# Attention scores of six heads by two stacked high/low products, with keys reloaded through DRAM in pieces

## The chip, the cores and the metric

The kernel runs on one core of a Trainium2 chip. The metric is device time in microseconds of one execution. The names of the engines are those of the profile: PE is TensorE (PEld its weight loads), DVE is VectorE, ACT is ScalarE, POOL is GpSimd, SP is the queue that issues most DMAs.

## The reference

A two-layer trunk on 1040 tokens (16 meta tokens and 1024 of input) of width 1024. The first layer has two groups of heads side by side; the change touches the first of them, eight heads of 64 with sparse attention:

```python
s = jnp.einsum('bqhd,bsd->bqhs', qib, k_idx)              # indexer of 16 heads picks the keys
score = jnp.einsum('bqhs,bqh->bqs', jax.nn.relu(s), wb)
_, idx = lax.top_k(jnp.where(causal, score, -inf), 256)
logits = einsum(q, k[idx]) * 64 ** -0.5 - slopes[h] * dist  # ALiBi
p = softmax(where(valid, logits, -inf)); out = einsum(p, v[idx])
```

The second group (HGRN2, eight heads of 64) is a gated linear recurrence over chunks. Both outputs go through one projection `w_out`, then DeepNorm layer norms, SwiGLU, and a second layer with pooling. Everything is in float32.

## The kernel before

Three stages follow one another with a barrier between them: `projection` (x by `w_in`, indexer scores, selection of 256 keys as a mask of distances, to about 466 us), `mixers` (both head groups and `w_out`, about 467 to 932 us) and `trunk` (all the rest). Selection is a mask, so the attention multiplies the queries of a tile with all keys up to it.

`mixers` walks nine tiles of queries: tile 0 has 16 rows, tiles 1 to 8 have 128 each, and tile m sees `NKEYS[m]` keys (16, 144, 272, 400, 528, 656, 784, 912, 1040). Each tile has eight steps, one for a head of attention (`units`) and at the same time one level of the recurrence. The order on every engine is written out in loops over `steps`; a step (m, h) puts on PE:

- `qk`: logits of head h (L1260), 128 queries by up to 1024 keys in float32, the head's 64 rows padded with zeros to 128 in `qaT` since `kaT` holds two heads in 128 rows; in tile 8 `qk_rest` does the last 16 keys;
- `gram` (L1303, L1293 at h = 0): products of the recurrence's level;
- a job in the `SHARED` bank of PSUM: `share` (h = 2, L1235), then `meta`, `out`, `kT`, `state`, `qa` for h = 0 to 4, `ot_rec` for h = 6. `qa` makes the queries of the next tile (L1196); in tile 0 it is spread over h = 0 to 3. Each use of the bank waits for `shared_done` of the use before it;
- `turn` (L1317): transposes of the probabilities of the head before; `pv_pair` (L1330) at odd h; a quarter of the output projection (`op`, L1253) at odd h.

DVE adds the mask to the logits and takes the maximum (`masked`, L1544; the next `qk` waits for `nmax_raw`), and copies the recurrence's products into `S`. ACT does the exponentials, the gates and most copies out of PSUM. POOL does `carry` (L1135, L1139): after `gram` of level h it scales `qp` and `key`, and `gram` of level h + 1 waits for it. `pT` has three buffers (`TS = 3`). SP's queue loads `z`, `q`, `v`, `g`, weights of `w_out` and rows of `y` in a written order. While PE has little to do in tile 0, `stream` issues products that nobody reads (L1349).

```python
            for a in range(0, min(NKEYS[m], 1024), 512):
                last = scores_of(m, h, a, min(512, NKEYS[m] - a), a)
            last.then_inc(qk_done, 1)
```

Of the kernel before, what the change touches and what calls it, by code (L numbers as in the profile page):

```python
# [12 lines left out]
P = 128  # L13
D = 1024
# [44 lines left out]
LEVELS = 7  # L59
SLOPES = [2.0 ** (-8.0 * (h + 1) / A_HEADS) for h in range(A_HEADS)]  # L60
# [23 lines left out]
def build(nc, ins, out):  # L84
# [3 lines left out]
    with ExitStack() as top:  # L88
# [19 lines left out]
        qz_dram = nc.dram_tensor("qz_scratch", [2, 4, P, L], F32, kind="Internal").ap()  # L108
        vg_dram = nc.dram_tensor("vg_scratch", [2, L, A_WIDTH], F32, kind="Internal").ap()
# [11 lines left out]
        with ExitStack() as heads:  # L121
            with ExitStack() as mixer:
# [6 lines left out]
                kaT = sb(mixer, "kaT", [P, 4, L])  # L129
                va = sb(mixer, "va", [P, NT, A_WIDTH])  # L130
                with stage() as c:
                    projection(nc, c, sem, sb, banks, ident, x, meta, w_in_v, ins, score, cqT, kaT, va, y, qz_dram, vg_dram, kiT, masks, w_qa0)
                with stage() as c:
                    mixers(nc, c, sem, sb, banks, ident, x, meta, ins, score, masks, w_qa0, cqT, kaT, va, y, qz_dram, vg_dram, raw, draw)
# [6 lines left out]
def projection(nc, c, sem, sb, banks, ident, x, meta, w_in_v, ins, score, cqT, kaT, va, y, qz_dram, vg_dram, kiT, masks, w_qa0):  # L141
# [75 lines left out]
    link = sem("dve_link")  # L217
    iota_done, w_qa_loaded, w_qa_scaled = sem("iota_done"), sem("w_qa_loaded"), sem("w_qa_scaled")
# [89 lines left out]
    def _(sp):  # L308
# [23 lines left out]
        for j, (col, _, _, _) in enumerate(SLABS):  # L332
            if j == 0:
                sp.wait_ge(x_transposed, NT)
            if j >= 2:
                sp.wait_ge(slab_hi, j - 1)
                sp.wait_ge(slab_lo, j - 1)
            if j == len(SLABS) - 2:
                sp.wait_ge(sc_psum, len(units))
            sp.dma_start(slab_raw(j), w_in_v[:, :, col:col + SW]).then_inc(slab_loaded[j % 2], 16)  # L340
            if j == len(SLABS) - 2:
                sp.dma_start(w_qa0, ins["w_uq"][0].rearrange("(k p) f -> p k f", p=P)).then_inc(w_qa_loaded, 16)

# [448 lines left out]
def mixers(nc, c, sem, sb, banks, ident, x, meta, ins, score, masks, w_qa0, cqT, kaT, va, y, qz_dram, vg_dram, raw, draw):  # L792
# [33 lines left out]
    u = sb(c, "u", [P, W])  # L826
    lnw = sb(c, "lnw", [P, W])
# [8 lines left out]
    q_past = sb(c, "q_past", [P, W])  # L836
# [4 lines left out]
    wq_last = [buf[:, i * DC * QW:(i + 1) * DC * QW].rearrange("p (k f) -> p k f", k=DC)  # L841
               for buf in (va[:, :, :].rearrange("p m f -> p (m f)"), kaT[:, :, :].rearrange("p f t -> p (f t)"))
               for i in range(2)]
# [28 lines left out]
    q_joined = sem("q_joined")  # L872

# [7 lines left out]
    def shared_job(m, h):  # L881
        jobs = {0: ("meta", m - 1), 1: ("out", m - 1), 2: ("kT", m - 1), 3: ("state", m - 1), 4: ("qa", m + 1), 6: ("ot_rec", m - 1)}
# [4 lines left out]
    def share_job(m, h):  # L887

        return m - 1 if h == 2 and 1 <= m <= NT else None

# [19 lines left out]
    assert shared_job(0, 4) == ("qa", 1) and not any(shared_job(0, h) for h in range(STEPS) if h != 4)  # L910
# [61 lines left out]
    def _(sp):  # L972
# [44 lines left out]

        load_z(0)
        load_q(0)
        sp.dma_start(w_qa[:, :, :], w_qa0).then_inc(w_loaded, 16)  # L1020
# [15 lines left out]
        for m in range(5):  # L1036
            load_y(m)
        for m, h in steps:
            if h == 0 and 1 <= m < NT - 1:
                load_q(m + 1)  # L1040
            if h == 5 and 1 <= m < NT:
# [8 lines left out]
            if (m, h) == (NT, 0):  # L1050
                sp.wait_ge(qk_done, NU)
                sp.wait_ge(qk_tail, A_HEADS)
            if (m, h) == (NT, 2):
# [1424 lines left out]
```

## Time and profile before

| what | value |
|---|---|
| median of 3 runs | 2519.51 us (2513.75 to 2519.68) |
| the profiled execution: its own time | 2521.23 us |
| span in its trace | 2519.4 us |
| PE busy | 2432.4 us (97%) |
| PE weight loads busy | 2081.2 us (83%) |
| DVE, ACT, POOL busy | 1177.1, 962.6, 1051.1 us |

The table reads: PE has something in flight nearly always, the other engines half of the time or less. Matmuls overlap in the array, so the distance between two starts tells the price of a product, not the duration in the row. The page cuts the span into 40 slices of 63 us; `mixers` fills slices 8 to 15.

### The profile page before, as it was taken

Reading aid. Unit: us, or ns where it says so; the run is one execution under the profiler, and the core shown is the slowest. Engines: PE = TensorE matmul, PEld = TensorE weight load, DVE = VectorE, ACT = ScalarE, POOL = GpSimd, SP = SyncE. Lnnn points to the kernel's source line nnn. Section 1 sums busy time; section 2 is a strip of 40 time slices with the busy share of each in tenths; the row PEclk is TensorE's granted clock in tenths of the full one; section 3 lists DMA queues with packets and bytes.
Section 4 is the critical chain, followed back from the end, with each engine's and each line's share of the span. In section 5 each row is a group of like instructions: output and inputs, shape, how many; then the busy total and the mean of one; then the engine's idle time right before and its main releaser. Section 6 shows DMA issues by size and latency. Waiting matters only on the chain.

```text
span 2519.4 us, 35989 instructions
## 1 busy us (share of the span) xinstructions
PE 2432.4 (97%) x13958; PEld 2081.2 (83%) x13958; DVE 1177.1 (47%) x2304; ACT 962.6 (38%) x1630; POOL 1051.1 (42%) x584
## 2 busy tenths in 40 slices
PE   7899999989999989999999999999999999999996
PEld 7889999767788779899898888888888888888885
DVE  6788985444455523333333466323355432232224
ACT  3677783334444324222223433322333322332222
POOL 0433123255554424443444544544544444455442
PEclk9999999899999999999999999999999999999998
DMA  4101330333333333333232323233233333333331
GB/s 140 34 18 35 100 100 31 105 97 114 101 113 106 103 111 117 92 101 97 72 101 84 100 71 114 84 117 89 79 101 101 87 97 101 100 101 103 115 101 42
DMA packets 275002, 231.42 MB, mean 92 GB/s; under 512 B 10769, under 2 KB 255569, under 8 KB 274833
## 3 DMA queue, kind: packets, MB, share of 16 engines
q1 hardware_dynamic: 266640, 220.59, 29.3%
q10 hardware_dynamic: 8192, 8.52, 1.0%
q8 instruction: 112, 1.84, 0.3%
q14 instruction: 58, 0.47, 0.1%
HBM read 215.81 MB, written 12.71 MB: 91 GB/s over the span
## 4 chain that ended last, share of the span: by engine, by line
PE 58%; DMA 1%; POOL 1%; ACT 1%; issue 1%; DVE 1%; POOLq 0%; SPq 0%; ACTq 0%; DVEq 0%
PE banks L2080 37%; PE banks L2114 19%; PE banks L2146 1%; DMA last_draw<-in_w_down 1%; POOL wL L2016 1%; PE banks L1801 1%; POOL dL L2023 1%; DMA cq_raw<-in_w_up 0%; PE banks L2105 0%; PE banks L2108 0%; PE banks L2132 0%; ACT wH L2192 0%; ACT dH L2198 0%; DVE y L2338 0%; ACT hH L1811 0%
## 5 line engine op out<-in xcount | busy, mean ns | idle before, releaser
L2016 POOL TENSOR_TENSOR wL<-cq_raw,wH 128x2048 fp32r<-128x2048 f32 x87 | 407.9, 4688 | 527.0 <-ACT wH L2192 527.0
L2080 PE MATMUL banks<-hL,wH 128*128 128x512 f32 (+1 forms) x1760 | 619.0, 352 | 7.7 <-ACT hid L2207 5.0
L2080 PE MATMUL banks<-hH,wL 128*128 128x512 f32 (+1 forms) x1760 | 618.1, 351 | 0.0
L2080 PE MATMUL banks<-hH,wH 128*128 128x512 f32 (+1 forms) x1760 | 616.1, 350 | 0.0
L2080 PEld LDWEIGHTS banks<-hL,wH 128*128 128x128 f32 x1760 | 331.3, 188 | 57.0 <-ACT hid L2207 6.3
L2312 DVE TENSOR_TENSOR hid<-hid,banks 128x512 f32<-128x512 f32 (+1 forms) x110 | 64.3, 584 | 656.3 <-PE banks L2080 554.8
L2080 PEld LDWEIGHTS banks<-hH,wL 128*128 128x128 f32 x1760 | 331.2, 188 | 46.3
L2080 PEld LDWEIGHTS banks<-hH,wH 128*128 128x128 f32 x1760 | 331.8, 189 | 45.0
L2023 POOL TENSOR_TENSOR dL<-last_draw,dH 128x1024 fp32r<-128x1024 f32 x88 | 220.2, 2502 | 313.7 <-ACT dH L2198 313.7
L2338 DVE TENSOR_TENSOR y<-y,banks 128x512 f32<-128x512 f32 (+1 forms) x340 | 231.9, 686 | 183.4 <-PE banks L2114 182.1
L2198 ACT ACTIVATE dH<-last_draw 128x1024 fp32r<-128x1024 f32 x88 | 93.3, 1060 | 498.7 <-PE banks L2114 321.3
L2114 PE MATMUL banks<-dH,hidL 128*128 128x512 f32 x704 | 278.8, 396 | 2.3 <-issue 2.3
L2114 PE MATMUL banks<-dL,hidH 128*128 128x512 f32 x704 | 277.9, 395 | 0.0
L2114 PE MATMUL banks<-dH,hidH 128*128 128x512 f32 x704 | 277.7, 394 | 0.0
L2209 ACT ACTIVATE hidH<-hid 128x512 fp32r<-128x512 f32 (+1 forms) x110 | 60.4, 549 | 384.7 <-DVE hid L2312 384.7
L2192 ACT ACTIVATE wH<-cq_raw 128x2048 fp32r<-128x2048 f32 x87 | 166.1, 1909 | 49.8 <-DMA cq_raw<-in_w_up 39.0
L2114 PEld LDWEIGHTS banks<-dH,hidL 128*128 128x128 f32 x704 | 132.5, 188 | 34.7 <-issue 2.7
L2114 PEld LDWEIGHTS banks<-dH,hidH 128*128 128x128 f32 x704 | 132.6, 188 | 31.3
L2114 PEld LDWEIGHTS banks<-dL,hidH 128*128 128x128 f32 x704 | 132.6, 188 | 30.5
L1135 POOL TENSOR_TENSOR qp<-qp,tot 64x256 f32<-64x256 f32 x112 | 77.2, 689 | 182.3 <-PE banks L1303 177.9
L501 PE MATMUL banks<-shared,hH 128*128 128x256 f32 (+1 forms) x648 | 136.9, 280 | 0.0
L501 PE MATMUL banks<-shared,hL 128*128 128x256 f32 (+1 forms) x432 | 120.7, 280 | 0.0
(278 smaller groups left out, 4074.8 us busy)
## 6 DMA issues: line engine op xcount, KB each, us to landing
cq_raw<-in_w_gate SPq DMA_DIRECT2D x88, 512.0 KB, 4.7
cq_raw<-in_w_up SPq DMA_DIRECT2D x88, 512.0 KB, 6.0
last_draw<-in_w_down SPq DMA_DIRECT2D x88, 512.0 KB, 3.4
w_out_part<-in_w_out SPq DMA_DIRECT2D x60, 512.0 KB, 4.0
va<-in_w_in SPq DMA_DIRECT2D x10, 1024.0 KB, 5.3
va<-in_x SPq DMA_DIRECT2D x8, 512.0 KB, 4.5
vg_scratch<-y ACTq DMA_DIRECT2D x32, 128.0 KB, 1.7
y<-in_x SPq DMA_DIRECT2D x8, 512.0 KB, 8.0
```

The source lines that it names most:

```text
L501: last = nc.tensor.matmul(banks[0:n, bank, 0:SW], h[:, k, a:a + n], w[:, k, :], start=first, stop=stop)
L1135: nc.gpsimd.tensor_tensor(late, late, blocks[r, :, 0, :].to_broadcast([HD, n, 2 ** l]), ALU.mult)\
L1801: last = self.nc.tensor.transpose(self.banks[:, self.bank_of(i), k * P:k * P + n], self.y[0:n, m, kk * P:(kk + 1) * P], self.ident[0:n, 0:n])
L2016: nc.gpsimd.tensor_tensor(wL[:, ff % 2, :, :, :].rearrange("p g k f -> p (g k f)"), raw[:, :, :, :].rearrange("p g k f -> p (g k f)"), wH[ ...
L2023: nc.gpsimd.tensor_tensor(dL[:, ff % 2, :], draw, dH[:, ff % 2, :].bitcast(F32), ALU.subtract)\
L2080: last = nc.tensor.matmul(banks[:, GU + (2 * q + g) % 3, 0:n], wt[:, ff % 2, g, k, :], h[:, k, a:a + n], start=(k == 0 and part == 0), sto ...
L2114: last = nc.tensor.matmul(banks[0:n, DN + num % 3, :], h[:, (2 * g + u) % 3, t0 - ph.t0:t0 - ph.t0 + n], wt[:, u, (j % 2) * 512:(j % 2 + 1 ...
L2192: nc.scalar.activation(wH[:, ff % 2, :, :, :], raw[:, :, :, :], ACT.Copy).then_inc(w_hi, 2)
L2198: nc.scalar.activation(dH[:, ff % 2, :], draw, ACT.Copy).then_inc(d_hi, 1)
L2209: nc.scalar.activation(hidH[:, ff % 3, a - ph.t0:a - ph.t0 + n], hid[:, q % 2, 0:n], ACT.Copy)\
L2312: nc.vector.tensor_tensor(hid[:, q % 2, 0:n], hid[:, q % 2, 0:n], banks[:, GU + (2 * q + 1) % 3, 0:n], ALU.mult)\
L2338: nc.vector.tensor_tensor(at, at, banks[0:n, DN + num % 3, :], ALU.add).then_inc(y_added, 1)
```

## The change

Six of the eight heads get their logits from two products in the reduced-width type fp32r. A head's key rows (64) are stored twice in 128 rows: the high part (rounded to fp32r) and the rest. The queries are also stored as two stationary matrices: `q_parts[0]` has the high part of q in both halves, `q_parts[1]` the rest of q over the half that meets the high keys and zero in the other. Two heads stay as they were, with `whole_keys`. The stacked keys of six heads need more room than `kaT`, and a shift across partitions, so the keys go to DRAM in `projection` and come back in `mixers`: the first 144 keys of six heads before the stage's end, the other 896 in three pieces of two heads, which ACT rounds (`keys_high`) and DVE subtracts (`keys_low`) at the steps (0,6), (1,1) and (1,4). Space is made by `TS = 2`, by `q_past` in `u`, and by other places for the last weights of `w_out`. The job `qa` is split in two (`qa` at h = 4, `qb` at h = 5), with the low parts made by DVE; `share` moves behind `qk` and `gram`.

```diff
+def load_keys(sp, raw_keys, k_dram, heads, at, signal):
+    for par in range(2):
+        for half in range(2):
+            sp.dma_start(raw_keys[HD * half:HD * (half + 1)].rearrange("p (f two) t -> p two f t", two=2)[:, par],
+                         k_dram[heads[0] // 2:heads[1] // 2, HD * par:HD * (par + 1), at].rearrange("f p t -> p f t")).then_inc(signal, 16)
...
+            if j == 6:
+                sp.wait_ge(slab_out, FILL_UNITS)
+                for f in range(4):
+                    sp.dma_start(k_dram[f], kaT[:, f, :]).then_inc(keys_stored, 16)
...
+        load_keys(sp, first, k_dram, (0, SPLIT_HEADS), slice(0, FIRST_KEYS), first_keys)
+        sp.wait_ge(first_keys, 64)
...
-    TS = 3
+    TS = 2
...
+    def piece_at(m, h):
+        return {(0, 6): 1, (1, 1): 2, (1, 4): 3}.get((m, h))
...
+        def load_piece(piece):
+            sp.wait_ge(k_split, piece)
+            part, heads, at = keys_in(piece)
+            load_keys(sp, part, k_dram, (heads.start, heads.stop), at, k_loaded)
+
         load_z(0)
         load_q(0)
+        sp.dma_start(whole_keys[:, :, :], k_dram[SPLIT_HEADS // 2:].rearrange("f p t -> p f t")).then_inc(kw_loaded, 16)
...
-        for m in range(5):
+        for m in range(3):
             load_y(m)
+        load_piece(1)
         for m, h in steps:
             if h == 0 and 1 <= m < NT - 1:
                 load_q(m + 1)
+            if piece_at(m, h) and piece_at(m, h) + 1 < KEY_PIECES:
+                load_piece(piece_at(m, h) + 1)
+            if (m, h) == (1, 7):
+                sp.wait_ge(k_split, KEY_PIECES)
+                load_y(3)
+                load_y(4)
...
+            if h < SPLIT_HEADS:
+                return nc.tensor.matmul(logits[0:n, at:at + kn], q_parts[:, part, h, 0:n], keys[:, h, a:a + kn],
+                                        start=(part == 0), stop=(part == 1))
...
+            if (m, h) == (0, 0):
+                pe.wait_ge(k_split, 1)
+            if m == 2 and h % 2 == 0 and h < SPLIT_HEADS:
+                pe.wait_ge(k_split, h // 2 + 2)
...
         for i, (m, h) in enumerate(steps):
-            if share_job(m, h) is not None:
-                on_shared("share", share_job(m, h))
             if i < NU:
                 qk(i)
...
             if m == 0 and h < 4:
-                on_shared("qa", 1, h)
                 stream(1)
-            if shared_job(m, h) and h and m:
+            if share_job(m, h) is not None:
+                on_shared("share", share_job(m, h))
+            if shared_job(m, h) and h:
                 on_shared(*shared_job(m, h))
...
+        def keys_high(piece):
+            if piece:
+                act.wait_ge(k_loaded, 64 * piece)
+            part, heads, at = keys_in(piece)
+            nc.scalar.activation(keys[:, heads, at], part, ACT.Copy).then_inc(k_hi, 1)
...
-            early = shared_job(m, h) if h == 3 else None
+            early = shared_job(m, h) if h in (3, 5) else None
...
+            if piece_at(m, h):
+                keys_high(piece_at(m, h))
...
+        def queries_low(what, m):
+            dve.wait_ge(q_hi, 1 if m == 0 else 2 * m + (what == "qb"))
...
+            last.then_inc(shared_done, 1)
```

PE in tile 4, steps 2 and 3, before. `rsums` is `share`, `ident,key` the job `kT`, `ident,probs` is `turn`; `k_tok` is the job `state`.

```order
L1235 MATMUL banks<-ident,rsums 64x128 x8
L1260 MATMUL banks<-kaT,qaT 128x512
L1260 MATMUL banks<-kaT,qaT 128x16
L1303 MATMUL banks<-qp,key 128x128 x4
L1204 MATMUL banks<-ident,key 128x128 x4
L1317 MATMUL banks<-ident,probs 128x128 x4
L1260 MATMUL banks<-kaT,qaT 128x512
L1260 MATMUL banks<-kaT,qaT 128x16
L1303 MATMUL banks<-qp,key 128x128 x4
```

The same place in the changed kernel, from `qk` of step 2 to `turn`:

```order
L1333 MATMUL banks<-keys,q_parts 128x512
L1333 MATMUL banks<-keys,q_parts 128x16
L1333 MATMUL banks<-keys,q_parts 128x512
L1333 MATMUL banks<-keys,q_parts 128x16
L1394 MATMUL banks<-qp,key 128x128 x4
L1308 MATMUL banks<-ident,rsums 64x128 x8
L1277 MATMUL banks<-ident,key 128x128 x4
L1408 MATMUL banks<-ident,probs 128x128 x4
```

`share` has moved from ahead of `qk` to right ahead of `kT`, which uses the same bank.

ACT at the end of tile 0 before, from the fifth head's exponentials of 16 rows:

```order
L1444 ACTIVATE tot<-lnw 128x512
L1404 ACTIVATE meta_probs<-probs 16x16
L1395 ACTIVATE probs,sums<-probs,nmax 16x16
L1404 ACTIVATE meta_probs<-probs 16x16
L1395 ACTIVATE probs,sums<-probs,nmax 16x16
L1404 ACTIVATE meta_probs<-probs 16x16
L1395 ACTIVATE probs,sums<-probs,nmax 128x144
```

The same place now; `keys<-y` is `keys_high(1)`:

```order
L1536 ACTIVATE tot<-lnw 128x512
L1494 ACTIVATE meta_probs<-probs 16x16
L1485 ACTIVATE probs,sums<-probs,nmax 16x16
L1585 ACTIVATE keys<-y 128x2x896
L1494 ACTIVATE meta_probs<-probs 16x16
L1485 ACTIVATE probs,sums<-probs,nmax 16x16
L1494 ACTIVATE meta_probs<-probs 16x16
L1485 ACTIVATE probs,sums<-probs,nmax 128x144
```

The copy of the first piece stands ahead of the last head's exponentials of tile 0 and of all of tile 1.

## Rows read from the trace of the kernel before

**Rows 1.** The page, part 1: busy us, share of the span, instructions.
```profile
PE 2432.4 (97%) x13958; PEld 2081.2 (83%) x13958; DVE 1177.1 (47%) x2304; ACT 962.6 (38%) x1630; POOL 1051.1 (42%) x584
```
**Rows 2.** Windows: us, busy us (instructions) by engine, PE clock, DMA share, GB/s.
```profile
490.00:510.00 20.00, 18.50 (x103) 17.42 (x102) 7.31 (x21) 5.26 (x20) 12.01 (x19) 0.51 0.42 145
510.00:528.00 18.00, 14.08 (x97) 10.06 (x96) 7.77 (x22) 8.20 (x30) 13.31 (x22) 0.98 0.21 57
```
**Rows 3.** Timeline of PE in tile 8: start, us, row.
```profile
853.32 1.88 PE L1260 MATMUL banks<-kaT,qaT 128*128 128x512 f32 x4
855.04 1.05 PE L1303 MATMUL banks<-qp,key 128*128 128x128 f32 x8
```
**Rows 4.** Timeline of PE in the indexer and in the trunk, fp32r products.
```profile
168.27 0.34 PE L477 MATMUL banks<-kiL,qiT 128*128 128x392 f32 x1
168.45 0.34 PE L479 MATMUL banks<-kiH,qiT 128*128 128x392 f32 x1
...
1499.61 0.39 PE L2114 MATMUL banks<-dH,hidL 128*128 128x512 f32 x1
1499.84 0.39 PE L2114 MATMUL banks<-dL,hidH 128*128 128x512 f32 x1
```
**Rows 5.** Timeline of PE, tile 4, from the op of step 1 to gram of step 3.
```profile
628.30 3.62 PE L1253 MATMUL banks<-w_out_part,oT 128*128 128x256 f32 x16
632.51 1.09 PE L1235 MATMUL banks<-ident,rsums 128*64 128x128 f32 x16 [0.58 <-DVE y L1630]
633.53 1.25 PE L1260 MATMUL banks<-kaT,qaT 128*128 128x512 f32 x4
634.63 1.16 PE L1303 MATMUL banks<-qp,key 128*128 128x128 f32 x8
635.63 0.60 PE L1204 MATMUL banks<-ident,key 128*128 128x128 f32 x4
636.06 0.60 PE L1317 MATMUL banks<-ident,probs 128*128 128x128 f32 x4
636.50 1.15 PE L1260 MATMUL banks<-kaT,qaT 128*128 128x512 f32 x4
638.40 1.13 PE L1303 MATMUL banks<-qp,key 128*128 128x128 f32 x8 [0.75 <-POOL key L1139]
```
**Rows 6.** Timeline of POOL at the same place: carry of level 2.
```profile
635.87 1.57 POOL L1135 TENSOR_TENSOR qp<-qp,tot 64x256 f32<-64x256 f32 x2 [9.79 <-PE banks L1303]
637.52 0.74 POOL L1139 TENSOR_TENSOR key<-key,tot 128x256 f32<-128x256 f32 x1
```
**Rows 7.** Waits of PE by line, 528 to 894 us: total, times, longest.
```profile
PE banks L1303 <- POOL key L1139: 4.8, 7, 1.5
PE banks L1235 <- DVE y L1630: 4.1, 7, 0.6
```
**Rows 8.** Timeline of PE, tile 4, steps 4 and 5.
```profile
646.37 1.14 PE L1303 MATMUL banks<-qp,key 128*128 128x128 f32 x8
647.35 1.95 PE L1196 MATMUL banks<-cq_raw,w_qa 128*128 128x128 f32 x16
...
650.57 1.14 PE L1303 MATMUL banks<-qp,key 128*128 128x128 f32 x8
...
653.60 3.72 PE L1253 MATMUL banks<-w_out_part,oT 128*128 128x256 f32 x16
```
**Rows 9.** Windows around the end of tile 0, columns as in rows 2.
```profile
482.00:494.00 12.00, 8.62 (x58) 6.33 (x57) 5.37 (x28) 6.46 (x25) 6.33 (x14) 0.85 0.93 300
494.00:496.00 2.00, 2.00 (x11) 2.00 (x11) 0.50 (x1) 0.31 (x2) 1.91 (x4) 0.50 1.02 402
```
**Rows 10.** Timeline: first product of tile 1 on PE; a copy into fp32r on ACT.
```profile
489.66 0.48 PE L1260 MATMUL banks<-kaT,qaT 128*128 128x144 f32 x2 [0.79 <-DVE nmax L1544]
...
245.94 1.92 ACT L514 ACTIVATE shared<-va 128x2048 fp32r<-128x2048 f32 x1 [0.46 <-ACT y L538]
```
**Rows 11.** Timeline of DVE: an operation of two operands in SBUF, 1024 elements.
```profile
847.26 1.22 DVE L1761 TENSOR_TENSOR y<-y,n_g 128x1024 f32<-128x1024 f32 x1
```

More of the change, by code:

```diff
@@ L909, in mixers @@
     shared = [("qa", 0)]
-    assert shared_job(0, 4) == ("qa", 1) and not any(shared_job(0, h) for h in range(STEPS) if h != 4)
+    assert shared_job(0, 4) == ("qa", 1) and not any(shared_job(0, h) for h in range(STEPS) if h not in (4, 5))
     for step in steps:
@@ L1189, in on_shared @@
             t0, n = TILES[m]
-            if what == "qa":
+            if what in ("qa", "qb"):
                 if m == 1:
@@ L1193, in on_shared @@
                 w = w_qa if m else w_qa0
-                for ft in q or range(4):
+                for ft in range(4) if m == 0 else range(2) if what == "qa" else range(2, 4):
                     for k in range(QC):
@@ L1238, in on_shared @@
                 last = quarter(m, *q, SHARED)
-            if what != "qa" or not q or q[-1] == 3:
-                last.then_inc(shared_psum, 1)
+            last.then_inc(shared_psum, 1)
         def quarter(m, q, bank):
@@ L1270, in qk @@
                     pe.wait_ge(nmax_tail, tails(i - 1))
-            for a in range(0, min(NKEYS[m], 1024), 512):
-                last = scores_of(m, h, a, min(512, NKEYS[m] - a), a)
+            for part in range(parts_of(h)):
+                for a in range(0, min(NKEYS[m], 1024), 512):
+                    last = scores_of(m, h, a, min(512, NKEYS[m] - a), a, part)
             last.then_inc(qk_done, 1)
@@ L1278, in qk_rest @@
             pe.wait_ge(nmax_raw, i + 1)
-            scores_of(m, h, 1024, NKEYS[m] - 1024, 0).then_inc(qk_tail, 1)
+            for part in range(parts_of(h)):
+                last = scores_of(m, h, 1024, NKEYS[m] - 1024, 0, part)
+            last.then_inc(qk_tail, 1)
         def gram(m, h):
@@ L1449, in off_shared @@
             src = banks[:, SHARED, :]
[L1450 to L1456 removed]
+            if what in ("qa", "qb"):
+                if m:
+                    act.wait_ge(qk_done, A_HEADS * (m - 1) + (4 if what == "qa" else 6))
+                if what == "qb" or m == 0:
+                    if m == 0:
+                        act.wait_ge(dve_pads, 3)
+                    for par in range(2):
+                        r = slice(HD * par, HD * (par + 1))
+                        nc.scalar.activation(q_whole[r, m % 2, par, 0:n], four(src)[r, 3, 0:n], ACT.Copy)
+                for par in range(2):
+                    r, other = slice(HD * par, HD * (par + 1)), slice(HD * (1 - par), HD * (2 - par))
+                    for to in (r, other):
+                        last = nc.scalar.activation(q_part(what, m, 0, par)[to], q_source(what, m)[r], ACT.Copy)
+                last.then_inc(q_hi, 1)
+                return
             if what == "share":
@@ L1489, in _ @@
             gates(0, stage)
+        keys_high(0)
         off_shared("qa", 0)
@@ L1568, in turned, with keys_low @@
                                       banks[:, T_HI, 0:k * P].rearrange("p (f t) -> p f t", f=k)).then_inc(t_dve, 1)
+        def keys_low(piece):
+            dve.wait_ge(k_hi, piece + 1)
+            part, heads, at = keys_in(piece)
+            for par in range(2):
+                r = slice(HD * (1 - par), HD * (2 - par))
+                k = keys[r, heads, at].rearrange("p (f two) t -> p two f t", two=2)[:, par]
+                raw_k = part[r].rearrange("p (f two) t -> p two f t", two=2)[:, par]
+                last = nc.vector.tensor_tensor(k, raw_k, k.bitcast(F32), ALU.subtract)
+            last.then_inc(k_split, 1)
+        def queries_low(what, m):
+            dve.wait_ge(q_hi, 1 if m == 0 else 2 * m + (what == "qb"))
+            if m == 0:
+                dve.wait_ge(dve_pads, 2)
+            for par in range(2):
+                r = slice(HD * par, HD * (par + 1))
+                last = nc.vector.tensor_tensor(q_part(what, m, 1, par)[r], q_source(what, m)[r],
+                                               q_part(what, m, 0, par)[r].bitcast(F32), ALU.subtract)
+            last.then_inc(shared_done, 1)
         def inverted(m):
```

102 lines of the change are left out of this document (74 added, 28 removed).

## The prediction

> **What bounds the kernel now.** I read the page's busy times first [rows 1]: PE has work in 97% of the span, the others in less than half, so a shorter product on PE is worth its time unless something else is late at that place. The change touches `mixers` alone (467 to 932 us), so the rest was read there. The windows [rows 2] show that this is not one regime: from 490 to 510 us, which is tile 1, the granted clock is 0.51 (the 1.2 GHz level) while PE is recorded busy for 18.50 of 20 us; later in tile 1 it is 0.98 and PE is busy for 14.08 of 18. The timeline of PE [rows 5, 8] shows the large tiles: products stand end to end and PE waits for 0.6 or 0.7 us at two places of a tile. The waits by line say how often: seven times for POOL's `carry` and seven times for a DVE addition ahead of `share`, 4.8 and 4.1 us over tiles 2 to 8 [rows 7]. So tiles 2 to 8 are bound by PE with a POOL chain close behind, tile 0 by handovers, tile 1 by a slow clock and by POOL.
>
> **The product.** A score against 1024 keys in float32 takes 855.04 - 853.32 = 1.72 us from start to start [rows 3], 1.68 ns for a key. The indexer's products are of the new kind, high and low keys in fp32r with other weights each time: 0.18 us for 392 columns, and 0.23 us for 512 in the trunk [rows 4], 0.45 ns for a column. Two of them cost 0.91 ns for a key, so 0.77 ns is saved. Tiles 2 to 8 see 272 + 400 + 528 + 656 + 784 + 912 + 1040 = 4592 keys; by six heads and 0.77 ns this is 21.2 us. Not shown is an fp32r product of 16 or 144 columns (tiles 4, 5 and 8 have 36). In tile 4, 528 keys take 634.63 - 633.53 = 1.10 us [rows 5], of which 0.86 is 512 keys, so a product of 16 columns takes 0.12 now. It could cost nothing or, if short ones run at float32's pace, 0.24 for 144 columns: minus 4 to plus 2 us in all. I take 0.11, the row's: tile 4's score then takes 2 x 0.23 + 2 x 0.11 = 0.68 us, 0.42 less.
>
> **Steps 2 and 3: `share` moves.** In tile 4 it takes 10.10 us from the `op` at 628.30 to `gram` of step 3 at 638.40 [rows 5]. New order: op 3.62, score 0.68, gram 1.00, share 1.02, a new wait, kT 0.43, turn 0.44, score 0.68. The new wait: `kT` uses the bank of `share`, so it waits for ACT's copy of it; behind `kT` in PE's queue stand `turn` and the next score. The old cover (score and gram between the two) is gone. Its price isn't shown; the nearest is the wait behind a DVE operation, 0.58 us [rows 5]; an ACT copy of 512 elements is about a quarter of 1.92 us [rows 10] plus a fixed part. I take 0.9, with 0.5 and 1.3 as ends. Sum 8.8 us, so 1.3 is gained, of which 0.84 are the two scores. Is POOL late next? It needs 638.40 - 634.63 = 3.77 us from gram to gram [rows 5, 6]; the new order has 1.00 + 1.02 + 0.9 + 0.43 + 0.44 + 0.68 = 4.5 us of work there. So both old waits go (8.9 us) and 7 x 0.9 = 6.3 comes: plus 2.6 us over seven tiles.
>
> **Steps 4 and 5: `qa` in halves.** Here POOL is late next. From gram to gram it is 650.57 - 646.37 = 4.20 us now, with all of `qa` (1.8) inside [rows 8]. With half of it and a shorter score PE has 1.00 + 0.9 + 0.44 + 0.68 = 3.0 us, less than POOL's 3.77. So 0.43 is gained and 0.9 (`qb`) put behind. The `op` that stands 7.23 us behind gram 4 now [rows 8] then also waits for `qb`'s way out: six small ACT copies (about 1.3) and two DVE operations (0.5) behind its end at 3.77 + 1.0 + 0.9 = 5.7, which gives 7.7 to 7.9. Against the full saving of two scores (0.84) tile 4 gives back about 1.1; tiles 2 and 3 about 1.5 each, tiles 5 to 7 0.9 down to 0.4, tile 8 has no such job. I take 5.5 us, ends 3 and 8.
>
> **Steps 0 and 1.** `gram` 1 waits for two DVE copies behind gram 0, and `out` for a chain on ACT that begins at the score of step 0; the first score's saving moves these, the second's hardly. I take 2.5 us given back, ends 0 and 4. ACT gets later by the moved `share`, so that `state` waits in tiles 2 and 3: 0.8. Tiles 2 to 8: 21.2 + 2.6 - 5.5 - 2.5 - 0.8 = 15 us gained, ends 8 and 21.
>
> **Tiles 0 and 1: the pieces.** ACT takes `keys_high(1)` at the end of step (0,6) and stands there until the piece has landed; behind it in its queue are the last exponentials of tile 0 and all of tile 1, and DVE, then PE, wait for them. When does it land? SP issues it behind v, two weight halves, two norm rows and three tiles of y: 0.26 + 1.05 + 1.05 + 1.11 MB, with the piece's 0.92 (128 x 1792 x 4 bytes) 4.39 MB. The queue moved 300 GB/s for 12 us and 402 for 2 [rows 9], 3.60 + 0.80 = 4.40 MB by 496.0 us. Then come the copy of 1792 elements at 1.92/2048 [rows 10], 1.7 us, two DVE operations of 896 at 1.22/1024 [rows 11], 2.1 us, and a mask with handovers, 0.9. Tile 1's first score starts at 500.7 instead of 489.66 [rows 10]: 11.0 us lost (ends 4 and 15). Up to here nothing else counts: the removed parts of `qa` and the splitting of the first 144 keys lie ahead of that wait. Piece 2 is asked for at about 501 and needed some 10 us later, and ACT has time then: nothing. Piece 3 puts 1.7 us on ACT and 2.1 on DVE between two steps that POOL bounds at 3.4: 2.5 us (ends 0 and 5). The slow stretch of tile 1 gains about 2 us: shorter scores on PE, and `share` behind `gram`, which starts POOL earlier. Sum 11.5 us lost.
>
> **The clock.** It fell at about 490 us, in a stretch of 12 us in which PE stood still for 3.4 [rows 9], and rose at about 510. In the changed kernel PE is idle from 489 to 501, so it falls too, and I let tile 1 have the same slow work, 20 us from 501. The Trainium skill, "TensorE: Matmul & The Clock Gate" (What's actually happening), has it that a low clock is the resting state and that a spell of activity releases it; rows 2 show 0.51 over 20 us with PE recorded busy for 18.50, so busy time alone was not enough here. By that rule tile 1 would run at the 2.4 GHz level almost at once and some 8 us come back: 2508 us.
>
> **Edits at nothing.** Writing the keys to DRAM (2.1 MB) lies beside slab products, with PE the bound. The first 144 keys are loaded once the masks are done, 10 us before PE ends the stage; without that cover they cost 3 us. `TS = 2` lets a copy of `pT` wait for `pv_pair`, and the `op` of the same step (3.6 us) covers it. `whole_keys` (1.06 MB) goes in where the queue idles. The last weights of `w_out` are in other places, asked for at the same point.
>
> **Sum.** The profiled execution took 2521.2 us, 1.7 above the median. It gives 2521.2 - 15 + 11.5 = 2517.7, or 2516 against the median of 2519.5.
>
> **Rivals.**
> - The wait at (0,6) is short. The four DMAs of 64 rows may be served beside those of y and not behind them; then the piece lands by 490 to 492, 4 to 6 us are lost instead of 11, and with less given back at steps 4 and 5 the late gain is 19: about 2507. For it: PE has hardly a gap in tiles 5 to 8. Against: the DMA share is 0.93 and more in just that stretch [rows 9]. Chance 0.27.
> - The clock, on the slower side: it doesn't rise where it did. It rose in the run of 128-column products around `state` of tile 1, and the new order has less of that. If it stays at 1.2 GHz to the first `op` of tile 2, the 14.08 us of PE work from 510 to 528 [rows 2] take up to twice as long, POOL's waits cover a few, and about 12 us are lost: 2528. It makes the kernel slower from 3.5 us on, so from some 5 us of such work. Chance 0.20.
> - ACT waits for pieces 2 and 3 as well, and each wait holds PE for 4 us: 2524 to 2530, taken as 2528. Against: the queue is nearly empty after 500. Chance 0.06.
> - The change doesn't do what it says: two fp32r products with weights that change each time cost as much as float32. The late gain falls to 2, and the time is 2530. Rows 4 speak against it. Chance 0.02.
> - The clock returns early, the page's rule: 2508. Chance 0.05.
> - The forecast, 2516, 0.40; its own range is 2511 to 2522.
>
> Under 0.3% (7.6 us) a measurement here can't tell from no change. Faster by more, below 2512: the first and fifth rival and a little of the forecast, 0.33. Slower by more, above 2527: 0.23. Within: 0.44. The range for 8 in 10 is 2503 to 2530.
>
> **What would show it.** Right: PE idle for 9 us or more ahead of tile 1's first score, ended by DVE or ACT behind a DMA into `y`; a score of 1024 keys at 0.93 us; `kT` waiting for ACT for 0.9 us in seven tiles; `gram` 5 waiting for POOL in tiles 2 to 7; from tile 2's first score to tile 9's 15 us less than the 366 us now. Wrong: tile 1 starting before 496, a clock that rises after another amount of work than about 20 us, or a late gain outside 8 to 21.

## The result and the profile after

| | kernel before | changed kernel |
|---|---|---|
| median of 4 runs each | 2519.5 us (2513.8 to 2519.7) | 2543.2 us (2541.7 to 2545.0) |
| span of the profiled execution | 2519.4 us | 2541.0 us |
| mean granted clock | 0.989 | 0.982 |

The ratio is 1.0102, with a 95% interval of 1.0085 to 1.0118: about 24 us slower, where 2516 us was forecast. The page's busy times:

```profile
PE 2424.4 (95%) x13958; PEld 2088.0 (82%) x13958; DVE 1196.1 (47%) x2347; ACT 984.6 (39%) x1702; POOL 1056.1 (42%) x584
```

PE has 8 us less work [rows 1] in a span that is 21.6 us longer, so 30 us of idle time were added. Where they are is read by cutting the stage (`mixers`) at the first score of each tile, in the timeline of PE (us):

| stretch | before | after | more |
|---|---|---|---|
| to the stage's first product | 467.6 | 465.2 | -2.4 |
| from there to tile 1's first score | 22.1 | 36.1 | +14.0 |
| tile 1 | 38.0 | 41.2 | +3.2 |
| tiles 2 to 7 | 301.3 | 309.9 | +8.7 |
| tile 8 | 65.0 | 65.0 | 0.0 |
| tail of the stage and trunk | | | -2.0 |

Tiles 2 to 8 were to give 15 us and took 8.7. Waits of PE in the changed kernel, 543 to 917.5 us, columns as in [rows 7]:

```profile
PE banks L1269 <- DVE q_parts L1698: 9.4, 6, 2.3
PE banks L1325 <- DVE q_parts L1698: 5.5, 6, 1.6
PE banks L1333 <- DVE nmax L1656: 5.3, 6, 1.7
PE banks L1277 <- ACT oT L1560: 4.9, 7, 0.7
PE banks L1394 <- POOL key L1212: 4.5, 7, 1.4
```

L1269 is `qa` and `qb`, L1325 `op`, L1277 `kT`, L1394 `gram`. The first two lines are new: PE waits for DVE's low parts of the queries, 14.9 us. The seven waits ahead of `share` are gone, seven of 0.70 us ahead of `kT` have come, and POOL's wait was not removed but went to step 5. Steps 4 and 5 of tile 6, PE, then ACT, then DVE:

```profile
715.74 1.06 PE L1269 MATMUL banks<-cq_raw,w_qa 128*128 128x128 f32 x8
...
718.34 1.13 PE L1394 MATMUL banks<-qp,key 128*128 128x128 f32 x8 [0.24 <-POOL key L1212]
721.81 1.16 PE L1269 MATMUL banks<-cq_raw,w_qa 128*128 128x128 f32 x8 [2.34 <-DVE q_parts L1698]
722.80 0.71 PE L1408 MATMUL banks<-ident,probs 128*128 128x128 f32 x5
723.44 1.31 PE L1421 MATMUL banks<-pT,va 128*64 128x128 f32 x20
725.71 3.72 PE L1325 MATMUL banks<-w_out_part,oT 128*128 128x256 f32 x16 [0.96 <-DVE q_parts L1698]
```
```profile
718.77 0.63 ACT L1531 ACTIVATE key<-key_arg 128x512 f32<-128x512 f32 x1 [0.48 <-DVE key_arg L1725]
719.31 1.53 ACT L1554 ACTIVATE q_parts<-banks 64x256 fp32r<-64x256 f32 x4
```
```profile
717.60 1.13 DVE L1725 SCALAR_TENSOR_TENSOR key_arg<-zt,lnw 128x512 f32<-128x512 f32 x1 [0.28 <-issue]
718.77 1.41 DVE L1728 SCALAR_TENSOR_TENSOR lnw<-zt,lnw 128x512 f32<-128x512 f32 x1
720.11 0.70 DVE L1749 COPY_PREDICATED S<-kiT,banks 128x512 f32<-128x512 uint8 x1
720.70 0.28 DVE L1679 COPY pT<-banks 128x128 f32<-128x128 f32 x1
720.90 0.85 DVE L1698 TENSOR_TENSOR q_parts<-banks,q_parts 64x256 fp32r<-64x256 f32 x2
```

`qa` is done at 716.8, but its bank comes free at 721.8: DVE's low part stands behind two gates and two copies, ACT's copies behind a gate's exponential that itself waits for DVE. `qb` needs the same bank, and behind `qb` stand `turn`, `pv_pair` and `op`. In tile 3 such a gap is followed by the lower clock: `qb` takes 2.08 us instead of 1.16, `op` 4.42 instead of 3.72:

```profile
619.13 2.08 PE L1269 MATMUL banks<-cq_raw,w_qa 128*128 128x128 f32 x8 [1.27 <-DVE q_parts L1698]
...
623.61 4.42 PE L1325 MATMUL banks<-w_out_part,oT 128*128 128x256 f32 x16 [0.28 <-DVE q_parts L1698]
```

The start of the stage on PE, and what ACT does ahead of tile 1; (0,5) below means step 5 of tile 0:

```profile
477.40 1.05 PE L1394 MATMUL banks<-qp,key 128*128 128x16 f32 x8 [1.92 <-POOL key L1201]
478.29 2.06 PE L1440 MATMUL banks<-va,ident 128*128 128x512 f32 x2
...
490.19 2.08 PE L1269 MATMUL banks<-cq_raw,w_qa 128*128 128x128 f32 x8 [2.49 <-DVE q_parts L1698]
...
494.86 0.23 PE L1336 MATMUL banks<-whole_keys,q_whole 128*16 128x16 f32 x2 [2.43 <-DVE nmax L1656]
501.28 0.67 PE L1333 MATMUL banks<-keys,q_parts 128*128 128x144 f32 x2 [6.18 <-DVE nmax L1656]
```
```profile
497.06 1.70 ACT L1585 ACTIVATE keys<-y 128x1792 fp32r<-128x1792 f32 x1 [1.65 <-DMA y<-k_scratch]
```

The forecast wait for piece 1 is there (ACT takes the piece at 497.1 where 496.0 was computed, 501.3 for the first score where 500.7 was), though ACT itself stood for it only 1.65 us. But two more waits, of 2.49 and 2.43 us, stand ahead of it, and from 478 to 509 us every product takes twice as long. Windows, columns as in [rows 2], the first fence from the kernel before, the second from the changed one:

```profile
480.00:488.00 8.00, 6.47 (x44) 4.68 (x44) 2.83 (x14) 4.52 (x13) 2.73 (x9) 1.00 0.64 206
```
```profile
480.00:490.00 10.00, 7.70 (x33) 6.17 (x31) 3.12 (x12) 3.66 (x12) 1.45 (x6) 0.50 1.00 314
490.00:510.00 20.00, 10.61 (x60) 9.61 (x60) 7.31 (x24) 6.66 (x23) 9.70 (x13) 0.52 0.57 136
510.00:528.00 18.00, 13.27 (x105) 11.63 (x104) 12.07 (x24) 12.91 (x35) 12.01 (x14) 0.91 0.27 66
528.00:548.00 20.00, 15.80 (x89) 11.71 (x90) 10.25 (x27) 6.94 (x26) 12.17 (x20) 0.74 0.46 145
```

In windows of 2 us the clock rises at 509 us, falls at 516, rises at 519, falls at 529 and rises at 540: of tile 1's 41.2 us, 21 are at the 1.2 GHz level, in three spells.

### The profile page after: what moved, and what is told of

It reads as the page before. It is cut to its first block, busy times and chain, and to the rows that moved or that the text cites. A ratio compares the mean times of both kernels' runs of the same rounds, so it can differ in the third digit from the quotient of the medians.

```text
span 2541.0 us, 36158 instructions
## 1 busy us (share of the span) xinstructions
PE 2424.4 (95%) x13958; PEld 2088.0 (82%) x13958; DVE 1196.1 (47%) x2347; ACT 984.6 (39%) x1702; POOL 1056.1 (42%) x584
## 4 chain that ended last, share of the span: by engine, by line
PE 57%; POOL 1%; DMA 1%; ACT 1%; issue 1%; DVE 0%; POOLq 0%; SPq 0%; ACTq 0%; DVEq 0%
PE banks L2218 36%; PE banks L2252 19%; PE banks L2284 1%; DMA last_draw<-in_w_down 1%; POOL dL L2161 1%; POOL wL L2154 1%; PE banks L1939 0%; DMA cq_raw<-in_w_up 0%; PE banks L2243 0%; PE banks L2246 0%; ACT dH L2336 0%; PE banks L2270 0%; ACT wH L2330 0%; ACT hH L1949 0%; DVE y L2476 0%
```

## Experiments

Twelve kernels, in three groups of four; each group shared its runs of the kernel before, whose medians were 2517.8, 2517.3 and 2516.7 us (2519.5 for the changed kernel's own). Medians of two groups are therefore good to some 3 us against each other; the ratios take that out. Each name says what was done. Starts and tiles come from one traced execution of each kernel. The column of the start is the time from the stage's first product to tile 1's first score.

| run | median, us | ratio to before (95%) | start | tile 1 | tiles 2 to 7 |
|---|---|---|---|---|---|
| changed kernel | 2543.2 | 1.0102 (1.0085-1.0118) | 36.1 | 41.2 | 309.9 |
| pieces later | 2541.0 | 1.0088 (1.0074-1.0102) | 32.3 | 43.0 | 310.0 |
| queries free | 2521.0 | 1.0007 (0.9998-1.0016) | 39.0 | 38.2 | 287.5 |
| before, share moved | 2510.9 | 0.9971 (0.9959-0.9982) | 22.1 | 33.4 | 296.7 |
| queries early | 2549.2 | 1.0120 (1.0106-1.0133) | 36.8 | 43.9 | 312.8 |
| quarters | 2533.9 | 1.0067 (1.0052-1.0082) | 23.5 | 43.1 | 309.3 |
| at once | 2532.4 | 1.0058 (1.0044-1.0073) | 23.4 | 39.1 | 310.9 |
| quarters, queries free | 2509.1 | 0.9967 (0.9956-0.9978) | 21.2 | 40.9 | 293.5 |
| before, qa at step 4 | 2524.4 | 1.0026 (1.0016-1.0037) | 28.3 | 36.2 | 301.2 |
| no low queries | 2530.1 | 1.0057 (1.0044-1.0071) | 37.6 | 40.8 | 294.4 |
| keys direct | 2525.7 | 1.0041 (1.0028-1.0055) | 23.7 | 37.1 | 309.2 |
| filled steps | 2538.6 | 1.0090 (1.0076-1.0103) | 28.3 | 42.7 | 309.9 |
| share moved and hold | 2508.9 | 0.9966 (0.9954-0.9979) | 22.8 | 32.2 | 296.7 |

**Pieces later.**

```diff
-        return {(0, 6): 1, (1, 1): 2, (1, 4): 3}.get((m, h))
+        return {(1, 1): 1, (1, 4): 2, (1, 7): 3}.get((m, h))
```

> The changed kernel, with ACT and DVE taking pieces 1, 2 and 3 of the keys at steps (1,1), (1,4) and (1,7) instead of (0,6), (1,1) and (1,4); PE needs them from (2,0), (2,2) and (2,4) on. Changed kernel: 2543 us, tile 1's first score at 501.3 us, 36.1 us behind the start of the stage. Theory A (the start is lost because ACT stands at (0,6) for a piece that nobody needs before tile 2): tile 1's first score comes 24 us behind the start of the stage instead of 36, PE's wait of 6.2 us ahead of it is gone; of the 12 us about 3 come back as waits at (1,7) to (2,4). Time 2534, 9 less. Rival B (the 5.3 MB of loads are what delays it, wherever ACT takes them; or the clock stays low for the same amount of work): the wait goes to tile 1 or 2 and the time is 2540 or more.

The wait of 6.2 us went (0.35 is left), and only 3.8 us of the start with it, 1.8 of which tile 1 gave back. The start of this execution also holds 1.6 us that the edit can't have made: the products up to the first score of tile 0 took 8.8 us at the lower clock, where the thirteen other traces have 7.1 to 7.3. Theory A was wrong on the start, and so was B: it is not the loads. PE still waited for 2.49 and 2.44 us at (0,5) and (0,7), at a clock of 0.50.

**Queries free.** The same edit serves below.

```diff
+                    nc.scalar.activation(q_whole[0:HD, m % 2, 0, 0:1], four(src)[0:HD, 3 if what == "qb" else 1, 0:1],
+                                         ACT.Copy).then_inc(shared_done, 1)
+                    return
...
-                queries_low(*shared_job(m, h))
```

> The changed kernel, but in tiles 1 to 8 the products of the queries (qa, qb) are not copied out of the shared bank: one ACT copy of a single column stands for the four to six copies and DVE's two low parts. It leaves out the queries of tiles 1 to 8, the products are all there. Theory A (the late gain was lost because PE waits for ACT's copies and for DVE's low part ahead of qb and of op: 11.9 + 5.5 us of waits in tiles 1 to 8, and the granted clock falls behind them): the waits of qb and op vanish, POOL's wait ahead of gram 5 takes back 0.9 us in each of seven tiles, the clock in tiles 3, 4, 6 and 8 is 1.00. From tile 2's first score to tile 9's turn 375.0 us become 361. Time 2529, 14 less. Rival C (POOL's carry chain bounds these steps anyhow): POOL's waits grow by what the others lose, 370 or more, time 2538.

Tiles 2 to 7 fell by 22.4 us, more than the 14 expected and more than the two lines in the list of waits (14.9): the clock, 1.00 there where it was 0.98, and masks and copies that no longer queue behind the queries would be the rest; how it divides was not measured. POOL's wait ahead of `gram` hardly grew (4.5 to 4.8 us), which is against C.

**Before, share moved.** One part of the change alone, with DVE's order as the change has it.

```diff
-            if share_job(m, h) is not None:
-                on_shared("share", share_job(m, h))
             if i < NU:
                 qk(i)
...
+            if share_job(m, h) is not None:
+                on_shared("share", share_job(m, h))
...
+            if i < NU:
+                masked(i)
             if h == 2 and 1 <= m <= NT:
                 normed(m - 1)
-            if i < NU:
-                masked(i)
```

> The kernel before, with the share alone moved: PE takes share behind the score and gram of step 2, DVE takes the norm behind the mask, as the changed kernel does; float32 products, keys in place. Theory A: seven waits ahead of share and about six for POOL ahead of gram 3 go, seven waits of kT for ACT of 0.7 us come, as the changed kernel's trace shows: 8.9 - 4.9 = 4 us gained, 2515.5. Rival D (moving share behind gram delays ACT's copy and the norms, and costs): 2519.5 or more.

It gained 6.8 us by the medians, and the interval of its ratio excludes 1: 4.6 us in tiles 2 to 7, where the clock is 1.00 in both kernels. Its trace has 4.6 us less in tile 1 too, but that is not shown to come from the move: the clock rose in step 1, at 495 us, ahead of the first job that was moved (the second row), where the kernel before ran the same products and got it back only at 511. By the medians some 2 us are left for tile 1.

```profile
493.62 2.74 PE L1224 MATMUL banks<-vt,S 128*128 128x64 f32 x16
498.45 0.64 PE L1235 MATMUL banks<-ident,rsums 16*64 16x16 f32 x16
```
```profile
488.00:510.00 22.00, 18.84 (x145) 16.89 (x144) 11.32 (x32) 10.23 (x37) 16.07 (x24) 0.83 0.43 146
```

Its waits from tile 2 to tile 8 show the one that came, 0.7 us in each of seven tiles, and what is left of POOL's; the one ahead of `share` is gone:

```profile
PE banks L1204 <- ACT oT L1460: 4.9, 7, 0.7
PE banks L1317 <- ACT pT L1413: 1.5, 3, 0.6
...
PE banks L1303 <- POOL key L1139: 0.6, 2, 0.3
```

Without the split of `qa`, POOL's 4.8 us [rows 7] all but vanish; in the changed kernel they return at step 5.

**Queries early.**

```diff
-            early = shared_job(m, h) if h in (3, 5) else None
+            early = shared_job(m, h) if h in (3, 4, 5) else None
...
                 normed(m - 1)
+            if shared_job(m, h) and shared_job(m, h)[0] in ("qa", "qb"):
+                queries_low(*shared_job(m, h))
...
-            if shared_job(m, h) and shared_job(m, h)[0] in ("qa", "qb"):
-                queries_low(*shared_job(m, h))
```

> The changed kernel, with the queries' way out taken earlier: ACT copies at step 4 ahead of the exponential, as it does at step 5, and DVE takes the low part behind the mask and ahead of the gates and of the copies of S. Nothing is left out. Theory A (DVE's low part at step 4 stands behind 2.5 us of gates and 1.0 us of copies in DVE's queue, ACT's copies behind the gates' exponential): qb's wait at step 5 falls from 2.3 to 1.0 us or less in six tiles, 8 us less in all, time 2535. Rival E (the copies themselves are the length of the wait, or PE then waits for the mask and for S instead): 2541 or more.

Slower by 6 us: `qb`'s wait left the list, and `turn` and `op` wait instead, for what DVE and ACT now do later. In tile 6:

```profile
726.21 1.16 PE L1269 MATMUL banks<-cq_raw,w_qa 128*128 128x128 f32 x8
730.06 1.30 PE L1408 MATMUL banks<-ident,probs 128*128 128x128 f32 x5 [2.69 <-DVE pT L1679]
731.29 2.40 PE L1421 MATMUL banks<-pT,va 128*64 128x128 f32 x20
733.62 5.02 PE L1325 MATMUL banks<-w_out_part,oT 128*128 128x256 f32 x16
```

Behind the wait of 2.69 us the clock fell: 0.76 from 726 to 740 us, and `op` took 5.02 us. My expectation named the place in the queue as the price; rival E holds: at this step another order moves the wait and does not remove it.

**Quarters.** On top of pieces later; `w_qa` is loaded ahead of `whole_keys`, and the waits for the bank follow the new order (not shown).

```diff
+    def at_once(m):
+        return m <= 1
...
+        if at_once(m + 1):
+            del jobs[4]
+            jobs[5] = ("qa", m + 1)
...
             if m == 0 and h < 4:
+                on_shared("qa", 1, h)
                 stream(1)
```

> As the run with the pieces one slot later (2541 us; 32.3 us from the start of the stage to tile 1's first score, 22.1 in the kernel before), and the queries of tile 1 computed in quarters again, one in each of steps 0 to 3 of tile 0, as the kernel before does, with one way out of the shared bank at step (0,5); the load of w_qa is asked for ahead of whole_keys. Theory F (the start is lost because the four quarters were taken out of steps 0 to 3 and stand at (0,4) and (0,5) behind handovers: PE has gaps, the granted clock falls at about 480 us and the rest of tile 0 runs at the 1.2 GHz level): the clock stays at 1.00 up to 487 us, the waits of 2.5 and 2.4 us at (0,5) and (0,7) become one of 2 us or none, the 32.3 us become 24 to 25, time 2533. Rival G (POOL's wait of 2.1 us ahead of gram 2 lets the clock fall in any case): 29 us or more, time 2538.

The start fell from 32.3 to 23.5 us, the time by 7.1 (5.3 by the ratios, whose intervals overlap a little). From the first score of tile 0 on it is 23.5 to 16.2 us, so 7.3 of the 8.8 us belong to the edit. That is the missing part of the start. The piece that is now taken at (1,4), which is piece 2, still costs a wait of 3.30 us in tile 1; DVE splits it ahead of the mask that PE waits for:

```profile
518.35 2.52 DVE L1698 TENSOR_TENSOR keys<-y,keys 64x896 fp32r<-64x896 f32 x2 [1.03 <-ACT keys L1594]
```
```profile
522.31 0.85 PE L1344 MATMUL banks<-whole_keys,q_whole 128*128 128x144 f32 x2 [3.30 <-DVE nmax L1665]
527.10 2.05 PE L1402 MATMUL banks<-qp,key 128*128 128x128 f32 x8 [0.69 <-POOL key L1219]
```

**At once.** `at_once` is true for all tiles.

> As the run before it, and in all tiles all the queries of the next tile are one job at step 5 with one way out (the buffer of heads 4 and 5 is free there). Theory A (two ways out of the same bank in two steps cost PE 2.7 us a tile): qb's waits go, the wait ahead of op becomes 1.5 us, POOL's ahead of gram 5 1.3 us longer: 1 us a tile gained, 5 to 7 us in all, 2527. Rival (what counts is the length of the way out, seven ACT copies and three DVE operations, and it is as long as before): the wait ahead of op is 2.5 us or more, 2533 or more.

The medians differ by 1.5 us and the intervals overlap. `qb`'s waits went (8.5 us in the list of the quarters run), and `op`'s grew from 5.4 to 13.4 us, 2.0 in tile 6:

```profile
709.26 1.95 PE L1276 MATMUL banks<-cq_raw,w_qa 128*128 128x128 f32 x16
711.05 0.71 PE L1416 MATMUL banks<-ident,probs 128*128 128x128 f32 x5
711.69 1.31 PE L1429 MATMUL banks<-pT,va 128*64 128x128 f32 x20
715.00 3.72 PE L1333 MATMUL banks<-w_out_part,oT 128*128 128x256 f32 x16 [2.00 <-DVE q_parts L1707]
```

With one way out `op` waits for 13.4 us, with two `qb` and `op` wait for 13.9: it is the length of the way out (here 711.0 to 715.0) and not its number.

**Quarters, queries free.** Both edits.

> As the first run of this call (pieces later, quarters in tile 0), and without the queries' way out in tiles 1 to 8 (one ACT copy of one column; the queries of tiles 1 to 8 are left out). It is what the products can give when nothing of the start and of the queries is lost. Beside the kernel before with share moved (2511 us, 296.7 us for tiles 2 to 7) it differs in the products and in the splitting of the keys. Theory A: 287 us for tiles 2 to 7, 24 us to tile 1, 2505. If the product term of the prediction (16.4 us over tiles 2 to 7, 4.8 in tile 8) held, it would be 280 us and 2495. Rival (the products are hidden behind POOL anyway): 292 or more, 2511 or more.

2509.1 us, a little more than expected. Tiles 3 to 7 take the same as in queries free; tile 2 takes 48.8 us instead of 42.8, since the late pieces now hold it. In time the products bring nothing beside share moved alone (2510.9) that can be told here, even with the queries left out. In tiles 3 to 7 alone they do: 244.7 us against 253.5. Tile 2 (48.8 against 43.2) and tile 1 (40.9 against 33.4) take that back.

**Before, qa at step 4.**

```diff
-                on_shared("qa", 1, h)
                 stream(1)
-            if shared_job(m, h) and h and m:
+            if shared_job(m, h) and h:
```

> The kernel before, with the queries of tile 1 as one job at step (0,4) instead of a quarter in each of steps 0 to 3; nothing else. No keys through memory, no fp32r product. Theory F: PE's gaps in steps 0 to 3 let the granted clock fall at about 480 us; 22.1 us from the start of the stage to tile 1's first score become 27 to 29, time 2524. Rival H (keys_low and keys_high of the first keys, and DVE's and ACT's work on them, are what opens the gaps in the changed kernel): 23 us, time 2519.

No key moved and no product changed, and the kernel before became 7 us slower; the start took 28.3 us. PE waited for POOL once in tile 0, in step 2, and the clock was at the 1.2 GHz level from 480 to 488 us with PE recorded busy all the time:

```profile
478.39 1.81 PE L1303 MATMUL banks<-qp,key 128*128 128x16 f32 x8 [1.54 <-POOL key L1128]
480.04 2.05 PE L1349 MATMUL banks<-va,ident 128*128 128x512 f32 x2
```
```profile
480.00:488.00 8.00, 8.00 (x26) 4.92 (x27) 2.47 (x10) 2.05 (x7) 1.47 (x6) 0.50 0.91 273
```

**No low queries.**

```diff
-                last.then_inc(q_hi, 1)
+                last.then_inc(shared_done if m else q_hi, 1)
...
-                queries_low(*shared_job(m, h))
```

> The changed kernel (2543 us), without DVE's low parts of the queries of tiles 1 to 8: ACT's last copy hands the shared bank over. It leaves out those low parts; the products are all there. Leaving out ACT's copies as well gave 2521. Theory J (half of the way out is DVE: its place behind gates and copies of S, and a second handover): qb's wait falls from 2.3 to 1.4 us and op's from 1.0 to 0, 11 us gained, 2532. Rival K (DVE's queue is all of it, ACT's copies hide): 2523 or less. Rival L (ACT's copies are all of it): 2540.

13 us faster than the changed kernel (11 by the ratios), 15.5 in tiles 2 to 7: of the 22.4 us of the way out, DVE's part is two thirds, the clock that returned to 1.00 included. What is left of the waits from tile 2 to tile 8:

```profile
PE banks L1269 <- ACT q_parts L1554: 3.1, 6, 0.8
...
PE banks L1325 <- ACT q_parts L1554: 1.9, 3, 1.0
```

**Keys direct.** On top of quarters: pieces 1 to 3 go from memory straight to `keys`, `keys_high` and `keys_low` are left out for them, and the loads no longer wait for a piece to be split.

```diff
-            part, heads, at = keys_in(piece)
-            load_keys(sp, part, k_dram, (heads.start, heads.stop), at, k_loaded)
+            _, heads, at = keys_in(piece)
+            load_keys(sp, keys[:, heads, at].bitcast(F32), k_dram, (heads.start, heads.stop), at, k_loaded)
```

> As the run with pieces later and quarters in tile 0 (2534 us), with pieces 1 to 3 loaded straight into the tile of keys: the same 2.75 MB, no copy on ACT, no subtraction on DVE (this leaves out the splitting of the keys behind the first 144). Theory M (the splitting holds ACT and DVE in tile 1 and the start of tile 2 for 5 and 8 us, and PE waits for some of it: 3.3 us ahead of a score, more at steps 1 to 4): from tile 1's first score to tile 3's 89.1 us become 84, 2529. Rival N (the slow clock and POOL bound tile 1 and hide it, or the 2.75 MB of loads cost the same): 88 or more, 2533.

8.2 us faster (6.5 by the ratios); tile 1 takes 37.1 us instead of 43.1, tile 2 the same. The wait of 3.30 us is gone, and the clock in the 40 us from 510 us on is 1.00, where it was 0.58 to 0.93 in quarters from 510 to 540. So theory M: the splitting costs there, with the lower clock that follows its wait. That the loads cost little is argued: tile 1 takes 37.1 us with them, and 38.0 and 36.2 in before and in before with `qa` at step 4, which have none.

**Filled steps.** On top of pieces later: `stream(2)` instead of `stream(1)` in steps 0 to 3 of tile 0.

> As the run with the pieces one slot later (2541 us, 32.3 us to tile 1's first score), with one more product of ident and v, whose result is not read, in each of steps 0 to 3 of tile 0, in the place of the quarters; the queries of tile 1 stay at (0,4) and (0,5). Theory F (the gaps let the clock fall): the clock stays at 1.00 to 488 us, the 32.3 become 27 to 28, 2536. Rival O (it is the handovers at (0,5) and (0,7), not the clock, that cost the 9 us): 31 or more, 2540.

The start took 28.3 us. The clock was 1.00 from 480 to 488 us, and the waits of 2.49 and 2.43 us were still there. From tile 0's first score to tile 1's it is 21.0 us, against 23.5 in pieces later and 16.2 in quarters: of the 7.3 us that the quarters brought, 2.5 come with the clock (the fillers' own time taken off), and the other 4.8 with the handovers and the work at (0,4) and (0,5). In the whole time no gain is shown: the ratio is 1.0090, and 1.0088 in pieces later.

```profile
480.00:488.00 8.00, 6.72 (x40) 4.50 (x39) 2.64 (x11) 4.68 (x16) 2.54 (x9) 1.00 1.00 315
488.00:500.00 12.00, 7.42 (x41) 6.41 (x42) 4.57 (x22) 5.32 (x24) 5.87 (x10) 0.57 0.80 193
```

**Share moved and hold.** On top of share moved: `stream(1)` in all eight steps of tile 0.

> The kernel before with share moved (2511 us), with one product of ident and v, whose result is not read, also in steps 4 to 7 of tile 0. In that run the clock fell at 488 us and rose at 493. Theory F: it stays at 1.00 over the start of tile 1, the added 2.2 us of work lie in PE's waits of 2.9 us there, 2 to 3 us gained: 2508. Rival: the added products stand in the way (2 us lost) or the clock falls later, in the waits for POOL in tile 1: 2511 to 2515.

2508.9 us, with the clock at 1.00 to 490 us and 0.91 from 490 to 510. It has the lowest median of all and beats both kernels, but its interval overlaps that of share moved alone, so what the added products bring is not shown.

## Why the prediction was wrong

Its 2516 us were 27 us too few. Step by step, as the prediction put them:

- **Steps 4 and 5: `qa` in halves, 5.5 us given back.** This is the step that failed. I wrote "So 0.43 is gained and 0.9 (`qb`) put behind", as if `qb` could start once `gram` 5 had been issued, and counted the way out of the bank only for the `op` behind it. But `qb` needs the bank that `qa` leaves, so it waits for the same way out, and I took that way as its durations alone (1.3 and 0.5 us), without what stands ahead of it in DVE's and ACT's queues: in tile 6 `qa`'s takes 5.0 us, from 716.8 to 721.8. The halving itself is not the price: at once has one way out and waits as long. Queries free prices the way out at 22.4 us over tiles 2 to 7, 17 more than the term; no low queries gives 15.5 of them to DVE. Share moved shows the other side: `qa` whole, with two ACT copies and no DVE, made PE wait for it nowhere.
- **The product, 21.2 us.** The mechanism was right, the size was not. A score of 1024 keys takes 1.11 us where I had 0.93, and 528 keys 0.79 where I had 0.68, against 1.72 and 1.0 to 1.1 before:

```profile
868.99 1.28 PE L1333 MATMUL banks<-keys,q_parts 128*128 128x512 f32 x4
870.10 1.07 PE L1394 MATMUL banks<-qp,key 128*128 128x128 f32 x8
```

  The medians by tile, from start to start where PE did not wait, give a saving of 0.20, 0.20, 0.25, 0.28, 0.41, 0.52 and 0.60 us for a score of tiles 2 to 8: 14.8 us with six heads, 6.4 less than the term. As a check, tiles 2 to 7 take 9.2 us less in queries free than in share moved, where these medians give 11.2. The pace of 0.23 us came from a stretch with hundreds of equal products; here four stand between products of another shape. I had the gap between such products in view only as the 16-column remainder.
- **`share` moved, 2.6 us gained.** Too low: 4.6 in tiles 2 to 7. In tile 1 the medians leave some 2 us, about what I had put there; the 4.6 of the trace lie beside a clock that rose before the move could act. The wait of `kT`, new, is 0.70 us (0.9 taken).
- **Tile 8.** The saving of its six scores, 3.6 us by the medians, came back in the same tile: the last 16 keys of a head wait for the mask over the first 1024, and a shorter first score hides less of it. That wait was 4.0 us in all before, and is 6.7 now. Another 1.6 went with a clock of 0.89 from 868 to 876 us: at 1.00, in queries free, tile 8 took 63.4 us.
- **Tiles 0 and 1, 11.5 us lost.** "Up to here nothing else counts: the removed parts of `qa` ... lie ahead of that wait" was wrong. The start lost 14.0 us. The piece's wait is 5.8 of them (6.18 where pieces later has 0.35); the quarters taken out of steps 0 to 3 are 7.3, and before with `qa` at step 4 shows 6.2 of them in the old kernel. That my 11.0 was near the sum was luck: without the piece tile 1 would have started at about 495.5 us, 8 us late already.
- **Pieces 2 and 3, 2.5 us.** They cost waits of 1.93 and 3.30 us in tile 1, and the clock fell again with both, at 516 and at 529 us. Keys direct puts the splitting at 6.0 us in tile 1. The rival that ACT waits for the pieces did not come about; it is the splitting that held.
- **The clock.** "the same slow work, 20 us from 501" was wrong in its course: it fell at 478 us already, rose at 509, 7.7 us after tile 1's first score, and fell twice more. That tile 1 had 21 us at the lower level in all, near the 20 forecast, was luck. What I had not looked at is what kept the clock high in tile 0: with the quarters beside the `stream` products it stayed at 1.00, without them it did not. Nor can its return be forecast from the products alone: behind tile 1's first score the same products brought it back after 21 us in the kernel before and after 8 us in share moved. The Trainium skill, "TensorE: Matmul & The Clock Gate" (What's actually happening), has it that activity releases the low clock. The traces here do not bear that out for recorded busy time: before with `qa` at step 4 stayed at 0.50 with PE recorded busy for 8.00 of 8 us.

The sum: 6.4 (product) + 16.9 (way out) - 2.0 (`share` in tiles 2 to 7) + 2.7 (tile 8's waits) is 24.0 of the 23.7 us between the 15 forecast and the 8.7 lost. The start adds 3.0 and tile 1 adds 2.7, and the stage before and the tail were 4.4 us shorter: 25 us, the profiled 2542.7 against the 2517.7 of the sum. The 4.4 us need no cause in the change: the four kernels of the old form, whose code is the same there, differ by 2.2 us in the first and by 3.3 in the second. That the rest closes to 0.3 us is luck in part: the terms for steps 0 and 1 (2.5) and `state` (0.8) were not tried by themselves, and tile 8's 1.6 us of clock are not in it. Nor were `TS = 2` and the places of `w_out`: tail and trunk together changed by 2 us at most, downwards.

The list of what would show it was useful: 1.11 instead of 0.93 us, `gram` 5 waiting for POOL, PE idle ahead of tile 1 (6.2 us, not 9) were all to be read, but PE's wait ahead of `qb` was not on it.

## What to carry to other kernels

A job that passes through a shared bank costs the way out of it, queues included, for whoever uses the bank next, whether that is one wait or two; an operand to be split into high and low parts puts two engines, one behind the other, on the way. Before work is taken out of a stretch in which PE has little to do, ask what else it did there: here the clock stayed up with it and fell without it. Try the small part of a change alone: moving one job behind two others brought 6.8 us, which the rest of the change had buried. And before a gain in a trace is put down to an edit, look whether the clock already differs ahead of the first instruction that the edit moved.

## What the runs showed of the hardware

- With one more product per step whose result nobody reads, the granted clock was 1.00 over 480 to 488 us, where it was 0.59 without (0.50 from 482 on), and tile 0 from its first score on was 2.5 us shorter for all the 3.4 us that four added products took (0.86 between starts). The time of the whole kernel did not show it.
- PE's wait for POOL in step 2 of tile 0 was followed by the 1.2 GHz level where it was 1.54, 1.92 and 2.12 us (before with `qa` at step 4, changed kernel, pieces later), in the first with PE recorded busy for 8.00 of the 8 us from 480; where it was 0.78 and 0.99 us (before, quarters) the clock stayed. In tile 6 a gap of 2.34 us was not followed by it. One trace each.
- The same products in the same order brought the clock back 21 us after tile 1's first score in one execution (before) and 8 us after it in another (share moved).
- Short runs of fp32r products do not reach the pace of long ones: 1.11 us for four of 512 columns between other shapes, 0.92 (four times 0.23) at the trunk's pace.
